# Loading a quarter of the cache pages through GpSimd's queue in the compression stage of a sparse-attention decoder layer

## What is computed

```python
def compress(x_raw, pe, w):          # blocks of 32 tokens, 2 kv heads of 64 channels
    xb = x_raw.reshape(B, Tk // 32, 32, N_KV, HEAD_DIM) + pe[:, None, :]
    return jnp.einsum('bnlgd,lde->bnge', xb, w)

k = rmsnorm(compress(kc_raw, pe[0], w[0]), k_norm_c)
v = compress(vc_raw, pe[1], w[1])
...
past_kc = cc_l[page_table, :, 0].reshape(bs, -1, N_KV, HEAD_DIM)   # 512 pages of 128 tokens
past_vc = cc_l[page_table, :, 1].reshape(bs, -1, N_KV, HEAD_DIM)
```

## Time and profile before

| | |
|---|---|
| median of 3 runs | 4290.12 us (4289.74 to 4298.05) |
| the profiled execution | 4288.17 us, span of its instructions 4286.3 us |
| granted TensorE clock, mean over the span | 0.934 |
| PE busy in the span | 3773.1 us (88%) |
| DVE, ACT, POOL busy | 36%, 22%, 19% |
| DMA | 558.02 MB, mean 130 GB/s |

### The profile page before, as it was taken

The page is one execution under the profiler, slowest core; times in us unless marked ns, Lnnn a source line. Parts: engine busy times, 40 slices in busy tenths (PEclk is TensorE's granted clock), DMA queues, the critical chain, the costliest instruction groups (busy, mean ns, idle before and its releaser), DMA issues. The chain is left out here.

```text
span 4286.3 us, 64338 instructions
## 1 busy us (share of the span) xinstructions
PE 3773.1 (88%) x23270; PEld 3191.8 (74%) x23270; DVE 1556.0 (36%) x3867; ACT 941.9 (22%) x2029; POOL 818.9 (19%) x969
## 2 busy tenths in 40 slices
PE   8999997534689999996379999999999999999998
PEld 6888885434466776765368888888888888888887
DVE  4344341010666666552013223432234322432223
ACT  1000000000356666653002111221022100221012
POOL 1010100000254323121002122221222211222112
PEclk9999998777799999997569999999999999999999
DMA  4101005666565443222234555645556555555553
GB/s 166 43 13 55 21 15 172 213 191 196 146 165 139 114 114 102 77 65 77 72 129 142 152 151 169 183 140 151 152 163 179 152 151 152 167 155 152 151 152 109
DMA packets 372823, 558.02 MB, mean 130 GB/s; under 512 B 55655, under 2 KB 155808, under 8 KB 371369
## 3 DMA queue, kind: packets, MB, share of 16 engines
q1 hardware_dynamic: 320984, 502.54, 40.5%
q10 hardware_dynamic: 50697, 43.79, 3.4%
q0 software_dynamic: 864, 7.85, 0.5%
HBM read 480.28 MB, written 78.50 MB: 130 GB/s over the span
## 5 line engine op out<-in xcount | busy, mean ns | idle before, releaser
L319 PE MATMUL ps_z<-x_gained,w_in_sb 128*128 128x257 f32 x2816 | 620.5, 380 | 20.6 <-DVE x_gained L355 20.6
L319 PEld LDWEIGHTS ps_z<-x_gained,w_in_sb 128*128 128x128 f32 x2816 | 533.0, 189 | 102.5 <-issue 21.6
L1746 PE MATMUL ps_tx<-ff,w_ring 128*128 128x257 f32 x1280 | 305.1, 380 | 7.8 <-DVE ff L1894 7.8
L980 ACT ACTIVATE PT_pr<-ps_p 128x384 f32<-128x384 f32 (+4 forms) x576 | 256.6, 496 | 243.6 <-PE ps_p L927 219.5
L1746 PE MATMUL ps_ty<-ff_sums,w_ring 128*128 128x257 f32 x1280 | 305.3, 380 | 0.0
L1746 PE MATMUL ps_ty<-h_sums,w_ring 128*128 128x257 f32 x1280 | 304.2, 379 | 0.2 <-issue 0.2
L1746 PE MATMUL ps_tx<-h_gained,w_ring 128*128 128x257 f32 x1280 | 303.3, 379 | 0.0
L1746 PEld LDWEIGHTS ps_tx<-ff,w_ring 128*128 128x128 f32 x1280 | 242.6, 190 | 44.3 <-issue 8.2
L1746 PEld LDWEIGHTS ps_ty<-ff_sums,w_ring 128*128 128x128 f32 x1280 | 243.1, 190 | 36.8
L1746 PEld LDWEIGHTS ps_ty<-h_sums,w_ring 128*128 128x128 f32 x1280 | 242.2, 189 | 36.7 <-issue 0.6
L1856 POOL TENSOR_TENSOR h<-h,u 128x257 f32<-128x257 f32 x192 | 135.4, 705 | 696.2 <-DVE u L1983 305.8
(11 more groups left out here) (291 smaller groups left out, 5442.4 us busy)
## 6 DMA issues: line engine op xcount, KB each, us to landing
w_ring<-scratch_w_sums SPq DMA_DIRECT2D x640, 256.0 KB, 2.6
w_ring<-in_w_tail SPq DMA_DIRECT2D x480, 256.0 KB, 2.6
w_blocks_pr<-in_w_tail SPq DMA_DIRECT2D x40, 1024.0 KB, 8.2
scratch_w_sums<-w_blocks_pr SPq DMA_DIRECT2D x40, 1024.0 KB, 5.4
pages<-in_cache_cmp SPq DMA_DIRECT2D x256, 128.0 KB, 3.5
pages<-in_cache_cmp ACTq DMA_DIRECT2D x256, 128.0 KB, 3.8
w_in_sb<-in_w_in SPq DMA_DIRECT2D x22, 512.0 KB, 13.8
x_chunk<-in_xT SPq DMA_DIRECT2D x16, 514.0 KB, 6.9
```

The costliest lines, as they stand in the source:

```text
L319: mm = pe.matmul(o, wg[:, k] if name == "g" else win[:, m, k], aT[:, c % 2, k, h * HF:(h + 1) * HF], start=(k == 0), stop=(k == KT - 1))
L980: act.activation(PT[0:rows, turn_no[x] % 3, g, 0:128 * w], tbank(k, g)[0:rows, 0:w], ACT.Copy).then_inc(s_cp, 1)
L1746: mm = pe.matmul(bank[:, 0:HF], w[:, k], b, start=(name in ("P1", "P6", "P5") and k == 0), stop=(name in ("P2", "P4", "P3") and k == 3), s ...
```

## The change

Each buffer's 32 pages are now shared by three engines: SP takes pages 0 to 11 and ACT pages 12 to 23, each in two groups of 6, and POOL takes pages 24 to 31 in one group of 8. POOL's DMAs count on a semaphore of their own, `s_pp[b]`, and PE waits for both counts. On POOL the pages of iteration 0 come after the three constants and ahead of the store of the bias line, and those of iterations 1 to 7 come after the load of the band.

```diff
+        s_pp = [ctx.enter_context(nc.semaphore(f"cp_software_pages{b}")) for b in range(2)]
...
-        HALF, AT_ONCE = NPG // 2, 8
+        SHARES = ((0, 12, 6), (12, 12, 6), (24, 8, 8))
 
         def load_pages(eng, side, i):
 
             for b in range(2):
                 eng.wait_ge(s_done[b], ONE + i)
                 plain(eng)
-                with eng.Fori(0, HALF // AT_ONCE) as j:
-                    base = j * AT_ONCE + HALF * side
+                first, n_pages, at_once = SHARES[side]
+                with eng.Fori(0, n_pages // at_once) as j:
+                    base = j * at_once + first
                     pages = [eng.value_load(ptab[0:1, ds(i * (2 * NPG) + (base + (NPG * b + x)), 1)], min_val=0,
-                                            max_val=d["cache_cmp"].shape[0] - 1) for x in range(AT_ONCE)]
+                                            max_val=d["cache_cmp"].shape[0] - 1) for x in range(at_once)]
                     for x, page in enumerate(pages):
                         eng.dma_start(pg[b][:, ds(base + x, 1)].rearrange("p a k n -> p (a k) n"),
-                                      d["cache_cmp"][ds(page, 1)].rearrange("a p k n -> (a p) k n")).then_inc(s_pg[b], 16)
+                                      d["cache_cmp"][ds(page, 1)].rearrange("a p k n -> (a p) k n")).then_inc((s_pp if side == 2 else s_pg)[b], 16)
...
                 pool.dma_start(cmask[:], d["cmask"]).then_inc(s_cm, 16)
+                pool.wait_ge(s_c, ONE + 16)
+                load_pages(pool, 2, 0)
                 pool.wait_ge(s_line, 3)
                 pool.dma_start(d["line"], line[:]).then_inc(s_st, 16)
...
                 pool.dma_start(t["band"][:], src).then_inc(s_band, 16)
+                with pool.Fori(0, NIT - 1) as i:
+                    load_pages(pool, 2, i + 1)
...
-                        pe.wait_ge(s_pg[b], ONE + 16 * NPG * (i + 1))
+                        pe.wait_ge(s_pg[b], ONE + 16 * 24 * (i + 1))
+                        pe.wait_ge(s_pp[b], 16 * 8 * (i + 1))
```

## The result

The changed kernel takes 4222.79 us (median of 4 runs, 4215.53 to 4223.62) against 4289.93 us: a ratio of 0.9844, 95% interval 0.9828 to 0.9859, or 67 us less. The profiled execution took 4223.62 us with a span of 4221.9 us, 64.4 us under the span before.

The account below looks back on a forecast made before the run. SP and ACT's issuing was taken to bound `compress`: 803 + 6 x 34.8 + 13.5 = 1025.3 us in place of 1081.3, so -56 us from the profiled 4288.2, plus 2 us to the median: 4234 us, range 4212 to 4285.

Parts of the forecast that it names:

- The pace: Steady iterations of `compress`: 34.8 us each with ACT the later queue (SP 34.1 us), 9.7 us less than before.
- What must fit under it: Per iteration of 34.8 us: PE's 22 us and transfers of 27.1 us fit, with no wait for a free buffer.
- POOL's price: POOL's queue in `compress`: 1.5 us per page DMA, between 0.58 and 2.3; eight pages 12.0 us, or 17.8 with numbers.
- The lower end of the sum: Whole kernel at POOL's low price of 0.58 us per page: -70 us, against -56 us at 1.5 us.
- Its 789: End of buffer 0's chunk in iteration 1 at 0.58 us per page: 789 us, against 803 at 1.5 us.
- The order on POOL: Start of `compress`: bias line out at 733 us, iteration 1's pages behind the band's load, landing near 794, chunk ending at 803.
- The head start: SP and ACT finish iteration 1 early, then wait for the late chunk; iterations 2 to 7 start from the old place.
- The long wait that I named as a sign: SP and ACT in `compress`: one long wait for a free buffer near 780 to 803 us, and none after.
- POOL as the slowest: Rival in `compress`: POOL slowest of three at 18.4 us per buffer, yet faster overall: -23 us, 4267 us; chance 0.17.
- POOL slower than before: Rival in `compress`: POOL's queue becomes the bound at 24.2 us per buffer: +59 us, 4349 us; chance 0.15.
- The price from which POOL decides: POOL in `compress`: from about 20.5 us per buffer on, the slower rival decides.
- a common limit: Rival in `compress`: issuing on three queues only slows each, so the pace stays: 4290 us, within 5 us; chance 0.10.

Follow-up runs that it names:

- the first experiment: Changed kernel, but POOL loads its pages in iteration 0 alone, a quarter of the cache unread in iterations 1 to 7: 4219.12 us.

## Why the prediction was right, and where it was off

*The bound.* SP's and ACT's sequencers are full of reading numbers and issuing. Right, and shown: with half the reads the pace falls to 33.0 us with no third queue, and with shares in between it lands in between. The reading of the earlier trace rows was no evidence for it, though: the 17 ns of that row stand there also after a long wait. In the kernel with 10, 10, 12 in one group each the same row of SP and its list of waits from 764 to 980 us are:

```profile
L2036 SPq EVENT_SEMAPHORE  x13: 17/17/17, 770.2 to 963.9; - x13
```

```profile
SPq L2036 <- PE ps_cmp L575: 48.9, 10, 7.6
```

What bears the claim are the runs just named, and that before the change the list of waits names none for SP from 760 to 1068 us.

*The pace.* Forecast 34.8 us with ACT as the later queue; measured 34.3 to 34.5 with ACT as the later queue. Right.

*What must fit under it.* Right but for a trifle: no wait for a free buffer on ACT, 4.7 us in all on SP from 764 us on.

*POOL's price.* This is the mis-sized term. I took 1.5 us for handing on a page, between 0.58 and 2.3; it is 0.60, the lower end. The landings of the small constants, 1.9 to 2.3 us apart, were no measure of the queue's own time per DMA: with 16 pages per buffer the queue took one every 0.62 us inside a group. The row that told the price was the duration of `cmask`. The Trainium skill says (Perfetto Trace Analysis, "DMA Instruction — SWDGE (GPSIMD)") that such an interval ends when the descriptors have been written; the trace agrees, since the pages landed a median of 2.7 us after their issue in that run while POOL went on every 0.62 us. The numbers are not read beside the DMAs: in that run POOL reads from 823.3 on, when the DMAs from 818.40 on have all been handed on, and issues again from 829.55. The lower end of the sum, -70 us, was the nearer one. Its 789 does not come out of the steps that give 825 at 2.3 us; at 0.58 us they give 784, and -75 us.

*The order on POOL.* I had the bias line at 733 and the pages of iteration 1 landed near 794, held behind the band's load. The line went out at 719.67 and the band's load at 754.39. The pages of iteration 1 went out from 768.88, and POOL began to read their numbers at 763.2, when the first chunk had ended at 762.9 and set their buffer free, in step with SP and ACT. The band did not hold them: by the DMA view it landed 14.0 us after its issue, at 768.4. Whether pages issued before that would have waited behind it no run shows. Line 485 from 755 to 769 us:

```profile
L485 POOLq TENSOR_LOAD <-page_table_sb x8: 283/288/302, 763.2 to 767.6; - x8
...
L485 SPq TENSOR_LOAD <-page_table_sb x6: 262/268/272, 763.3 to 767.0; - x6
...
L485 ACTq TENSOR_LOAD <-page_table_sb x6: 273/276/292, 763.9 to 767.3; - x6
```

So the first chunk of iteration 1 ended at 794.0 and not at 803. That is 9 of the 11 us by which the stage gained more than forecast (67.5 against 56); the pace gave some 6 x 0.5 = 3 us.

*The head start.* I said that SP and ACT would be through iteration 1 early and then lose it to the band. There was no head start to lose: the first chunk came 4.5 us later than before, with the transfers full at 316 GB/s. I had the 4.5 MB copy behind the first pages; since POOL's pages were cheap it went out at 732.48, landed 21.6 us later by the DMA view, and so still ran while PE waited for the first buffer until 752.87. The long wait that I named as a sign, near 780 to 803, is not there; SP's longest, 8.7 us, ends with the first chunk. The step's result was nearly right (iteration 2 starts from the old place), its reason was not. In the run with SP and ACT alone in iteration 0 the time and the pace are the same, so the start holds none of the gain.

*The gain as a whole.* It reached the end of the kernel: the stages behind differ by 3 us in 3200.

*The rivals.* POOL as the slowest, and POOL slower than before, were both real mechanisms, at 12 and 16 pages per buffer in two groups. The price from which POOL decides, 20.5 us per buffer, was right in kind: at 16 pages it took 22.9 us, half of 45.8, and the kernel was slower than before. The rival "a common limit" fell with the first experiment. The Trainium skill's rule in DMA: Bandwidth & Descriptors, "Issuing engines are not separate DMA queues", holds in its first half, since a third queue saved sequencer time and nothing else; that this time is small beside the transfer does not hold for 128 KB pages whose numbers are read one by one (1.29 us of SP's time against an estimated 0.42 us at 310 GB/s).

## What to carry to other kernels

An engine that only reads registers and issues DMAs shows as idle in the busy times. Read its sequencer's rows, and if the list of waits names none for it and its loop step does not change, its own instructions are the bound; then price one item, and moving items to another queue is worth that price times their number until the next queue or the transfers are full. When the destination queue has no row of that item, price all of it there (number, gap, hand-over) and expect the balance to shift back as soon as that queue has no idle time left: 8 pages on POOL cost nothing, 12 in groups of six made it the bound, 16 lost the gain and more. Before adding queues, look at what is done per item: half the reads of the page table brought the pace lower (33.0 us) than the third queue did (34.3 us).

## What was not expected

A page number has no fixed price. In one group per buffer it costs 0.62 to 0.65 us on SP and ACT and 0.64 us on POOL, in two groups 0.68 to 0.74 us and 0.71 us. Why is not shown; what differs in the program is the number of rounds that the loop over groups makes. On POOL each group also pays nearly a microsecond between its last number and its first DMA. Both are parts of why shares of 10, 10 and 12 take 4201.64 us in one group each and 4218.17 us in two. POOL's page DMAs land a median of 3.8 us after their issue, against 3.1 and 2.8 us on the hardware queues of SP and ACT, by the DMA view of the changed kernel from 764 to 1006 us:

```profile
pages<-in_cache_cmp SPq DMA_DIRECT2D x168, 128.0 KB, 3.1
pages<-in_cache_cmp ACTq DMA_DIRECT2D x168, 128.0 KB, 2.8
pages<-in_cache_cmp POOLq DMA_DIRECT2D x112, 128.0 KB, 3.8
```

That is no fixed property of the queue. With shares 8, 8 and 16 the order turns round, 2.7 us on POOL against 3.7 and 3.8 us on SP and ACT (790 to 1068 us).
